# Eight of 24 modulation units moved from TensorE matmuls to VectorE row products

## The reference

```python
def modulation(cond, w_ada, b_ada):
    m = jax.nn.silu(cond) @ w_ada + b_ada
    return [t[..., None, :] for t in jnp.split(m, 6, axis=-1)]
...
    for i in range(DEPTH_2):
        sh1, sc1, g1, sh2, sc2, g2 = modulation(c, w_ada[i], b_ada[i])
        csh1, csc1, cg1, csh2, csc2, cg2 = modulation(c_ctx, w_ada[i], b_ada[i])
        h = modulate(rms_norm(x, norm1_g[i]), sh1, sc1)
        hc = modulate(rms_norm(ctx, norm1_g[i]), csh1, csc1)
```

## Time and profile before

| | |
|---|---|
| three runs, median (lowest to highest) | 1656.63 us (1656.02 to 1659.84) |
| the profiled execution | 1655.9 us, span 1654.1 us |
| mean granted TensorE clock in it, as a share of full | 0.995 |
| ring loads, 1 MB each, of `w_ada` for PE | 24 |
| the same of `w_ada_rows` for DVE | 24 |
| stage: hybrid block | about 15 to 504 us |
| stage: first feed-forward, up units | about 504 to 635 us |
| stage: first feed-forward, down units | about 635 to 701 us |

### The profile page before, as it was taken

The page is one execution under the profiler, slowest core; times in us unless marked ns, Lnnn a source line. Parts: engine busy times, 40 slices in busy tenths (PEclk is TensorE's granted clock), DMA queues, the critical chain, the costliest instruction groups (busy, mean ns, idle before and its releaser), DMA issues.

```text
span 1654.1 us, 34573 instructions
## 1 busy us (share of the span) xinstructions
PE 1596.3 (97%) x14802; PEld 1448.0 (88%) x14802; DVE 1215.8 (74%) x2069; ACT 881.4 (53%) x1344; POOL 189.4 (11%) x120
## 2 busy tenths in 40 slices
PE   8999999999999999999988999999999998799999
PEld 7999888898999999998867888888887897699999
DVE  4375499687877886588866788876888779568864
ACT  5435645548546665456775444323433456666653
POOL 4303540000000110100000011101110000041100
PEclk9999999999999999999999999999999999999999
DMA  7655555464455554531202243463435333045554
GB/s 280 249 215 227 195 219 183 169 230 179 145 187 179 184 191 158 182 109 54 76 2 74 107 153 128 146 232 142 155 136 207 110 103 103 3 157 200 202 167 143
DMA packets 41129, 259.67 MB, mean 157 GB/s; under 512 B 4368, under 2 KB 7696, under 8 KB 14480
## 3 DMA queue, kind: packets, MB, share of 16 engines
q1 hardware_dynamic: 40976, 257.46, 43.6%
HBM read 256.39 MB, written 1.05 MB: 156 GB/s over the span
## 4 chain that ended last, share of the span: by engine, by line
PE 68%; DVE 23%; ACT 4%; issue 2%; DMA 2%; DVEq 0%; SPq 0%; ACTq 0%
PE acc_psum L209 20%; PE acc_psum L210 19%; PE acc_psum L211 19%; DVE w_low_sb L174 5%; DVE mod_products L336 3%; DVE u_filtered L2116 2%; DVE ring_sb L336 2%; PE acc_psum L218 2%; DMA ring_sb<-in_w_up 1%; ACT w_high_sb L162 1%; PE acc_psum L2609 1%; DVE norm_rt_sb L1848 1%; PE acc_psum L272 1%; ACT norm_rt_sb L2869 1%; PE acc_psum L2638 1%
## 5 line engine op out<-in xcount | busy, mean ns | idle before, releaser
L209 PE MATMUL acc_psum<-h_high_sb,w_high_sb 128*128 128x256 f32 (+1 forms) x2176 | 655.8, 301 | 5.1 <-DVE h_low_sb L502 1.9
L210 PE MATMUL acc_psum<-h_low_sb,w_high_sb 128*128 128x256 f32 (+1 forms) x2176 | 647.9, 298 | 0.0
L211 PE MATMUL acc_psum<-h_high_sb,w_low_sb 128*128 128x256 f32 (+1 forms) x2176 | 647.9, 298 | 0.0
L162 ACT ACTIVATE w_high_sb<-ring_sb 128x1024 fp32r<-128x1024 f32 (+2 forms) x412 | 387.0, 989 | 359.3 <-PE acc_psum L211 212.5
L174 DVE TENSOR_TENSOR w_low_sb<-ring_sb,w_high_sb 128x1024 fp32r<-128x1024 f32 (+1 forms) x362 | 395.7, 1135 | 103.4 <-ACT w_high_sb L162 93.8
L209 PEld LDWEIGHTS acc_psum<-h_high_sb,w_high_sb 128*128 128x128 f32 x2176 | 411.1, 189 | 32.4 <-issue 12.7
L210 PEld LDWEIGHTS acc_psum<-h_low_sb,w_high_sb 128*128 128x128 f32 x2176 | 409.0, 188 | 15.5 <-issue 0.5
L211 PEld LDWEIGHTS acc_psum<-h_high_sb,w_low_sb 128*128 128x128 f32 x2176 | 408.8, 188 | 15.0
L2116 DVE SCALAR_TENSOR_TENSOR u_filtered<-acc_psum,par_sb,u_filtered 128x255 f32<-128x255 f32 (+2 forms) x264 | 150.7, 571 | 48.0 <-ACT u_filtered L2257 29.5
L2293 POOL TENSOR_TENSOR u_low<-u_filtered,u_high 128x256 fp32r<-128x256 f32 (+1 forms) x66 | 67.3, 1020 | 956.3 <-ACT u_high L2286 956.3
L209 PE MATMUL acc_psum<-u_high,w_high_sb 128*128 128x256 f32 (+1 forms) x539 | 169.7, 315 | 4.5 <-DVE w_low_sb L174 2.8
(11 more groups left out here) (310 smaller groups left out, 1875.4 us busy)
## 6 DMA issues: line engine op xcount, KB each, us to landing
ring_sb<-in_w_in SPq DMA_DIRECT2D x68, 1024.0 KB, 6.4
ring_sb<-in_w_up SPq DMA_DIRECT2D x66, 1024.0 KB, 4.9
ring_sb<-in_w_down SPq DMA_DIRECT2D x48, 704.0 KB, 4.2
ring_sb<-in_w_ada SPq DMA_DIRECT2D x24, 1024.0 KB, 4.8
ring_sb<-in_w_ada_rows SPq DMA_DIRECT2D x24, 1024.0 KB, 4.9
ring_sb<-in_w_out SPq DMA_DIRECT2D x12, 1024.0 KB, 4.8
ring_sb<-in_w_br_hg SPq DMA_DIRECT2D x4, 1024.0 KB, 6.9
ring_sb<-in_w_br_ml SPq DMA_DIRECT2D x4, 1024.0 KB, 4.8
```

Of the source, the lines that this page charges most:

```text
L162: self.nc.scalar.activation(self.high[:, self.shifted(c, g, piece)], self.ring[:, c % RING, piece], ACT.Copy)\
L209: nc.tensor.matmul(out, sh, mh, start=start, stop=False)
L210: nc.tensor.matmul(out, sh, ml, start=False, stop=False)
L211: return nc.tensor.matmul(out, sl, mh, start=False, stop=stop)
```

## The change

Of layer 0's 24 units, 16 remain on PE and 8 become row products on DVE.

- `RIDES` is 19, 21 to 49: the nine rides behind units 1 to 17 go, one behind unit 49 comes. All 16 are joined at once (`TOGETHER` 16) and read at iteration 53.
- Row slots stand behind units 3, 5, 7 and 9 of the hybrid block (`EARLY_RIDES`). DVE's loop takes each one in the iteration before, behind the low part of that unit.
- Four more stand behind down units 2, 5, 8 and 11 of the first feed-forward (`ROW_RIDES["first_down"]`), in halves: tile 0 of the slot in iteration r-1, tile 1 in iteration r, both behind the low part of the next unit and ahead of the residual.
- `cond_rows` is loaded at the start and once more between the hybrid block and the first feed-forward; ACT's activation of it comes at iteration 2 of the hybrid block's loop and at iteration 0 of the first down projection (`EarlyRows`), there between the high parts of units 1 and 2.
- The low parts of units q and f (but for unit 1, DVE's already), and those of the second layer's out projection and first up unit, go from POOL to DVE. The low part of unit 0 stands ahead of DVE's reciprocal of the first norm.
- The gains that `AttentionAhead` prepares for layer 0 read tiles of the four early row slots; the tiles of the four in the first down projection are used later. The weights of the eight units are laid out by rows on the host.

```diff
-LOW_BY_POOL = ("q", "f", "ml_qk", "xbc")
+LOW_BY_POOL = ("ml_qk", "xbc")
-RIDES = tuple(range(1, 2 * (N_ADA * P // UNIT), 2))
-ROW_RIDES = {"out": (1, 2), "up0": (1, 3, 4, 6, 7, 9), "down0": (0, 2, 3, 5, 6), "up1": (0, 2, 3, 5, 6, 8, 9), "down1": (0, 2, 3, 5)}
+RIDES = tuple(range(19,51,2))
+EARLY_ROWS = 8
+EARLY_RIDES = (3, 5, 7, 9)
+ROW_RIDES = {"first_up": (), "first_down": (2, 5, 8, 11), "out": (1, 2), "up0": (1, 3, 4, 6, 7, 9), "down0": (0, 2, 3, 5, 6), "up1": (0, 2, 3, 5, 6, 8, 9), "down1": (0, 2, 3, 5)}
...
-    TOGETHER = 12
+    TOGETHER = 16
...
+class EarlyRows(Hook):
+    def act(self, act, n):
+        if n == 0:
+            self.rows.activate(act)
...
+    rows.hold(view(7 * W8, 2, D), rt[:, :].rearrange("p (a b) -> p a b", a=2))
+    rows.taken += len(EARLY_RIDES)
...
+            rows.fetch(sp, a["cond_rows"])
+            core.release(sp, UNITS, (mod, rows))
...
+                if n == 2:
+                    rows.activate(act)
...
+            core.split_low(dve, 0, "dve")
             norm1.reciprocal(dve)
...
+                if n + 1 in EARLY_RIDES:
+                    rows.dot(dve, EARLY_RIDES.index(n + 1), core.place(n + 1) + 1)
-                if n == 2 * NM + 2:
-                    mod.read(dve, NM // mod.TOGETHER)
+                if n == RIDES[-1] + 4:
+                    mod.read(dve, len(RIDES) // mod.TOGETHER)
...
-                if n in rides:
+                if n in rides and not both:
                     side.dot(dve, m0 + rides.index(n), core.place(g0 + n) + 1)
                 turned = norms and n == units - 1
                 if n and not turned:
                     core.split_low(dve, g0 + n + 1, "dve")
+                for j in range(2) if both else ():
+                    if n + 1 - j in rides:
+                        side.dot(dve, m0 + rides.index(n + 1 - j), core.place(g0 + n + 1 - j) + 1, (j,))
```

More of the change, by code:

```diff
@@ L15 @@
+import collections
 import itertools
@@ L104, in __init__ @@
         self.stream = []
-        self.released = self.sides = 0
+        self.released, self.sides = 0, collections.Counter()
         self.taken = 0
@@ L119, in phase @@
         yield self.block
-        self.sides = 0
+        self.sides.clear()
         for s in self.signals.values():
@@ L192, in release @@
             else:
-                self.sides += 1
-                sp.wait_ge(*side.multiplied.at(self.sides))
+                kind = self.stream[c][2]
+                self.sides[kind] += 1
+                sp.wait_ge(*{s.KIND: s for s in sides}[kind].multiplied.at(self.sides[kind]))
             self.load(sp, c + RING)
@@ new lines, in hold, with fetch, activate, result @@
+    def hold(self, rows, products):
+        self.rows, self.products = rows, products
+        self.begun.append(self.taken)
+    def fetch(self, sp, src):
+        sp.dma_start(self.rows.rearrange("p a b -> p (a b)"), src).then_inc(*self.rows_in.dma())
+    def activate(self, act):
+        act.wait_ge(self.rows_in.handle, 16 * len(self.begun))
+        self.core.nc.scalar.activation(self.rows, self.rows, ACT.Silu).then_inc(*self.rows_ready.one())
+    def result(self, n, j):
+        (bias, result), t = (self.early, N_ADA - 2 * EARLY_ROWS + 2 * n + j) if n < EARLY_ROWS else (self.layer, 2 * (n - EARLY_ROWS) + j)
+        return bias[:, t, 0:1], lambda s: result[:, t, s:s + 1]
@@ L333, in dot @@
+    def dot(self, dve, n, c, tiles=(0, 1)):
+        core, slot = self.core, self.core.ring[:, c % RING, :].rearrange("p (j k) -> p j k", j=2)
+        if 0 in tiles:
+            core.wait_loaded(dve, c)
+            if n in self.begun:
+                dve.wait_ge(self.rows_ready.handle, self.begun.index(n) + 1)
+            if n:
+                dve.wait_ge(self.multiplied.handle, n)
         for s in range(2):
-            for j in range(2):
-                t, row = 2 * n + j, slot[:, j, :]
+            for j in tiles:
+                row, (bias, result) = slot[:, j, :], self.result(n, j)
@@ L896, in build @@
             else:
-                add("w_up_2", range(up0, up0 + FFT), "dve", "pool", NARROW)
+                add("w_up_2", range(up0, up0 + FFT), "dve", "dve", NARROW)
                 add("w_down_2", range(down0, down0 + 2 * DT), "dve", "dve", NARROW)
-        assert counts == [NM, NM]
+        assert counts["columns"] == len(RIDES) and counts["rows"] == NM + EARLY_ROWS
         with nc.Block() as core.block:
@@ L932, in arena @@
                 core.arena = None
[L934 to L935 removed]
+            by_columns = slice(0, 2 * len(RIDES))
+            mod = Modulation(core, cond, select[:, :], pv("b_ada0", N_ADA)[:, by_columns], adaM[0][:, by_columns, :], mod_sums)
+            rows = RowModulation(core, *((pv(f"b_ada{i}", N_ADA), adaM[i]) for i in range(LAYERS)))
             norm2 = TokenNorm(core, "second", X, H, [Stream(0, lambda t: pr("norm2", t), None, core.norm_sq)], ident, 3, 7, (3, 3, 6))
             with arena("arena_hybrid"):
[L938 removed]
+                hybrid_block(core, a, X, H, pr, pv, cn, con, view, ident, causal, small, mod, rows, norm2)
             def norms_of(i):
@@ L987, in build @@
                     if side:
-                        rows.rows, rows.products = (held.enter_context(nc.sbuf_tensor(n, [P, 2, D], F32)) for n in (
-                            "cond_rows", "mod_products"))
+                        rows.hold(*(held.enter_context(nc.sbuf_tensor(n, [P, 2, D], F32))[:, :, :] for n in ("cond_rows", "mod_products")))
                     rest = out_projection(core, a, H, T, *joined, residual(2), norm2, core.eps[:, 0:1], side)
@@ L1006, in _, with hybrid_block @@
                 sp.wait_ge(store.stored.handle, 16 * DT)
-def hybrid_block(core, a, X, H, pr, pv, cn, con, view, ident, causal, small, mod, norm2):
+def hybrid_block(core, a, X, H, pr, pv, cn, con, view, ident, causal, small, mod, rows, norm2):
     nc, sig, psum = core.nc, core.sig, core.psum
@@ L1996, in _ @@
                     sp.wait_ge(handle, value)
-                sp.dma_start(side.rows[:, :, :].rearrange("p a b -> p (a b)"), a["cond_rows"]).then_inc(*side.rows_in.dma())
-            core.release(sp, g0 + units, side)
+                side.fetch(sp, a["cond_rows"])
+            core.release(sp, g0 + units, [side] if side else ())
         @block.tensor
@@ L2053, in _ @@
                 if side and n == 0:
-                    act.wait_ge(side.rows_in.handle, 16)
-                    core.nc.scalar.activation(side.rows[:, :, :], side.rows[:, :, :], ACT.Silu).then_inc(*side.rows_ready.one())
+                    side.activate(act)
                 if n >= 1:
@@ L2118, in feed_forward @@
         for p, first in enumerate(range(0, FFT, n)):
+            up_rides, down_rides = (ROW_RIDES[name] for name in (("first_up", "first_down") if seg == 1 else (f"up{p}", f"down{p}")))
             up(core, H, T, first, n, lambda ch: (cw(lead, ch), cb(ch)), conv3, tmp, uh, ul, None if p else norm,
-               up_banks, first_use, done_before, side, ROW_RIDES[f"up{p}"] if side else (), rest)
+               up_banks, first_use, done_before, side, up_rides if side else (), rest)
             free = core.sig("up_bank_free")
```

78 lines of the change are left out of this document (41 added, 37 removed).

## The result

The changed kernel takes 1665.9 us (median of 13 runs, 1660.1 to 1673.5) against 1658.5 of the kernel before beside it (13 runs, 1652.1 to 1663.4); the ratio is 1.0049, interval 1.0032 to 1.0066. It is slower by 5 to 11 us, where I forecast no difference and set the upper end at 1664. The forecast was 0.7 above the median of the three runs of before that I had (1656.63); against the 13 runs here the difference is 7.4.

A forecast was written before the change was run, and what follows sets the result against it. The prediction took TensorE, busy 97% of the span, to bound the kernel. Its terms -8.0 - 0.4 - 0.4 + 1.6 + 8.2 gave +1.0; it took 1657.3 us, no difference, with the range 1649 to 1664.

The forecast's parts named there:

- (b): First down projection: row slots freed late delay the loads of units three places on; +2.2 us.
- Rides off PE: Early units: nine rides of 1.00 us go and one comes, -8.0; joinings and copies -0.4.
- The start: Unit 0's low part on DVE delays the reciprocal, but h's first low part gets faster; -0.4 us, ends -0.6 and +1.1.
- DVE in the first units: Units 2 to 6: low parts, products and memsets on DVE make PE wait at unit 6; +1.6 us, ends 0 and 3.
- rival E: Clock falls to 0.57 for 4 us behind the two waits of (c); 1.7 us more, 1659; chance 0.04.
- Rival D: DVE binds the early units beyond unit 6, losing half of the 8.0; +3 to +4, 1660.5; chance 0.08.
- The first down projection: Half slots of 2.4 us on DVE delay PE through (a), (b) and (c); +8.2 us, ends +3 and +12.
- (a): First down projection, iteration 1: activation and half slot delay unit 3's low part, so PE waits; +2.1 us.
- (c): First down projection, iterations 10 and 11: half slots ahead of DVE's values delay units 12 and 13; +3.9 us.
- rival C: First down projection: late second halves delay loads, high and low parts and next products round the ring; about 1663; chance 0.17.

The follow-up runs named there:

- e10: e8 with 128 unused bytes a partition, which gives it the addresses of the kernel before; 1652.8 us, ratio 0.9972.
- e12: The kernel before with 32 unused bytes a partition ahead of `mod_sums` and no instruction changed; 1660.3 us, ratio 1.0020.
- e1: The changed kernel with row slots in the hybrid block only; the first down projection's four are rides on PE again; 1666.9 us, ratio 1.0050.
- e14: e10 with six row slots in the hybrid block (behind units 3 to 13) and 18 rides; 1658.5 us, ratio 1.0010.
- e13: e9 with 8 filler matmuls of 512 columns on a free bank ahead of PE's waits at down units 3, 12 and 13; 1673.3 us, ratio 1.0092.
- e8: e1 with the memsets and the cast moved from iteration 4 of DVE's loop to iteration 1; 1662.5 us, ratio 1.0019.
- e2: The changed kernel with row slots in the first down projection only, none in the hybrid block, and 20 rides; 1670.7 us, ratio 1.0060.
- e4: The changed kernel with the first down projection's half products moved to the end of each iteration; 1670.6 us, ratio 1.0068.
- e11: e10 with the low parts of q and f on POOL again; 1658.8 us, ratio 1.0017.
- e9: The changed kernel with 736 unused bytes a partition behind `cond_sb`, which restores the addresses of the kernel before; 1664.3 us, ratio 1.0040.
- e15: e10 unchanged, run again beside e14; 1655.2 us, ratio 0.9994.

## Why the prediction was wrong

Two steps failed. Term (b) of the first down projection, 2.2, rested on PE's waits giving the ring its time back; the runs showed a chain through the ring in which PE has no part, and a stage that is 11.2 longer in place of 8.2. And the sum had nothing for the addresses of the tensors, which cost 3.8 in stages that the change does not touch.

- **Rides off PE, -8.4: right, or a little small.** Units 2 to 18 lose the rides behind 1 to 15 and are 7.1 and 5.7 us shorter than the first trace of before in the two traces, with 2.3 and about 4.0 of wait and clock in them. In e10, where five rides are gone and no wait has come, they are 5.6 shorter, 1.1 a ride in place of 1.00.
- **The start, -0.4: a little off.** The reciprocal came at 12.78, not 12.4; the first low part of h took 0.43 (not 1.93), as worked out. At unit 2 the kernels with this start stand between -0.1 and +0.9 to the first trace, +0.4 in the mean, but e12, with the start of before, stands at +0.4 as well. Within its ends.
- **DVE in the first units, +1.6: mechanism right, 2.3 to 2.7 in size,** and behind it the clock fell in one of the two traces of the changed kernel and in e1 (about 1.7 and 3.4 us by the granted clock of their windows). I had the clock as rival E for the down projection only, and priced this wait without it. Rival D did not happen: in the changed kernel no unit from 7 to 28 waits; e14 shows that it would begin with the next slot, the one behind unit 11.
- **The first down projection, +8.2: the term that was mis-sized is (b).** The stage cost 11.2. (a) is 2.0 for 2.1, right. (c) came as 2.1 at unit 12 and 0.95 ahead of unit 13, 3.1 for 3.9 (the matmuls of the earlier trace rows, which I took for the starts of units 12 and 13, are those of units 11 and 12, and the high part of the earlier trace rows is unit 12's). What is left for (b) and for the clock behind the waits is about 6, where I had 2.2: from the first matmul of unit 1 to that of unit 12 the stage is 8.7 longer (54.0 for 45.4), and (a) and (c) are 4.1 of that. I chose, against my own rival C, to let PE's waits give the ring its time back. They can't: the chain is load, high part, low part, product and load again, and what PE does meanwhile is not in it. (Whether a fourth place in the ring would hide this was not tried.) Two pieces of it I had not named: the load of a row slot, 7.46, which I had down as the slot that costs least (I counted the down units' loads alone, 4.2), and a wait of 1.4 for norm sums, whose squares stand behind a high part that waits for its load.
- **Rival C** had the mechanism and nearly the stage's size (12.2 with its +4). As a difference it gave 6.4 (1663 for 1656.6), against 7.4 measured. I gave it 0.17 and put the range's end there. Rival E's sign was there too (0.78 behind unit 12), and behind unit 3 besides; of that first fall e13 got back 0.5 of 1.7.
- **Nothing in the sum stood for the addresses.** The change moved every tensor behind `cond_sb`, and this costs 3.8 us in the three down projections of the attention layers by the landmarks, 1 to 6 in e12's times. This was the cause that e1 exposed: with the down projection's products undone the kernel should have been 7 us faster than the changed one and was not. The wait at the memsets (4 by e8's median) and the addresses (the ratio falls by 0.0047 from e8 to e10, more than the down projections alone account for; e10's trace has the short first up projection, e8's the long one) make up what was missing there.
- **The scans scatter.** Units 28 to 44 vary from 127.6 to 139.1 over the traces (e1's is the longest). Part of that can be read off: the granted clock there is 0.99 on average in the first trace of before and 0.94 in e1's, some 7 us more by my estimate, and PE is idle for 10.8 us in place of 7.7, one of its waits for DVE being 5.7 long. Why one trace has more of this than another is open.

By its terms with measured sizes: -8.4 + 0.4 + 2.3 + about 1 (clock behind it) + 11.2 + 3.8 = +10.3, against 5 to 11 measured. That this falls inside is in part luck, since two differences are not in it that came in both pairs of traces: the first up projection was 4.2 shorter with the change, and the scans, by the two means, 3 longer. From unit 2 to unit 205 the two traces of the changed kernel are 8.7 and 4.2 longer than the two of before, in the order in which they were taken. The same terms give e2 +9.7 (6 to 14 measured), e1 +4 to +6 (5 to 11) and e10 -4 to -2 (-7 to -2). Whether the short first up projection belongs to the change is open (e12, the program of before 32 bytes on, has it too; e4, at the addresses of the change, has not).

## What to carry to other kernels

Where weights go through a short ring, an operation that holds a slot is priced with the whole loop behind it (release, load, split, and the loads that stand behind it in the queue), not with its own time, and a free share of its engine says little. A wait put on TensorE can cost its granted clock as well; of the one such fall that was tested here, most was covered by the chain. And keep the addresses when two kernels are compared: pad what a size change moves, or a difference of a fifth of a percent (e12's) may be that of an address.

## What was not expected of the hardware

At a granted clock of 1.00, TensorE's interval between matmuls of 256 columns is 113 or 118 ns, and of 512 columns 227 or 233, in stretches of up to 130 us (a first up projection of 125.8 or 130.0 us). In layer 1's up projection it differs between two traces of one program; the first up projection had 125.8 in both traces of the changed kernel and 130.0 in both of the kernel before, and in e8 to e12 one or the other (130.0 in e8 and e11), so what sets it there is open. In the down projections a shift of 32 bytes a partition of the tensors read (e12) brought the longer one in all three, and going back to the old addresses (e9) the shorter one; 128 and 736 bytes lower were slow too. In layer 1's the old addresses did not suffice (e10, e13, e15). Which property of the address does it was not tried.
